# Second pass of a hybrid decoder step: the transposes of the normed rows inside v's projection instead of in front of it

## The reference: what is computed

```python
def trunk_layer(x, p, conv_buf, C0, n0, m0, lp):
    mix, new_state = parallel_mixer(rmsnorm(x, g_mix), ...)   # mLSTM heads and chunk MLP, then W_out
    h = x + mix
    h = h + hier_moe(rmsnorm(h, g_ffn), ...)                  # routed experts
    h = h + jax.nn.sigmoid(h @ w_pg) * rmsnorm(p @ w_ple_l, ple_g)
    return h, new_state

def chunk_mlp(u, v, w_s_l, b_s_l, vn_g):
    vn = rmsnorm(jax.nn.gelu(v).reshape(B, L, G_B, DG_B), vn_g.reshape(G_B, DG_B))
    z = jnp.einsum('gts,bnsgc->bntgc', w, vn.reshape(...)) + b_s_l[:, :Lc].T[:, :, None]
    out = jax.nn.gelu(u) * z.reshape(B, L, W_B)
    return out, vn.reshape(B, L, W_B)
```

## Time and profile before

| | |
|---|---|
| median of three runs | 2383.95 us |
| the profiled execution, its own time | 2384.98 us |
| its span in the trace | 2383.4 us |
| TensorE busy (matmuls) | 2200.5 us, 92% |
| VectorE busy | 1491.1 us, 63% |
| ScalarE busy | 973.5 us, 41% |
| GpSimd busy | 466.9 us, 20% |
| DMA, mean over the span | 171 GB/s |
| mean granted TensorE clock | 0.957 |

### The profile page before, as it was taken

The page is one execution under the profiler, slowest core; times in us unless marked ns, Lnnn a source line. Parts: engine busy times, 40 slices in busy tenths (PEclk is TensorE's granted clock), DMA queues, the critical chain, the costliest instruction groups (busy, mean ns, idle before and its releaser), DMA issues. The chain is left out here.

```text
span 2383.4 us, 34278 instructions
## 1 busy us (share of the span) xinstructions
PE 2200.5 (92%) x10675; PEld 1809.1 (76%) x10676; DVE 1491.1 (63%) x2827; ACT 973.5 (41%) x1567; POOL 466.9 (20%) x617
## 2 busy tenths in 40 slices
PE   7999988999699999998398999999999999969998
PEld 5888877788578788887277888878888888747775
DVE  5787787877635544554545467486664666835654
ACT  4334332343422222222344457376654665723332
POOL 1121443221112322322100000000000000023332
PEclk9999988999899999998699999999999999989999
DMA  6102112112523322321577577698775779844331
GB/s 219 62 32 82 62 40 97 40 62 98 177 74 100 115 102 98 115 100 45 213 295 278 221 266 291 244 347 295 294 296 219 272 286 349 300 168 143 134 142 59
DMA packets 159158, 407.04 MB, mean 171 GB/s; under 512 B 18700, under 2 KB 22212, under 8 KB 158847
## 3 DMA queue, kind: packets, MB, share of 16 engines
q1 hardware_dynamic: 137350, 337.15, 39.1%
q0 software_dynamic: 14560, 43.11, 5.4%
q10 hardware_dynamic: 7200, 26.22, 2.7%
HBM read 330.10 MB, written 84.82 MB: 174 GB/s over the span
## 5 line engine op out<-in xcount | busy, mean ns | idle before, releaser
L1961 DVE TENSOR_TENSOR w_lo<-raw,w_hi 128x2048 fp32r<-128x2048 f32 x196 | 434.9, 2286 | 49.0 <-ACT w_hi L1897 49.0
L1897 ACT ACTIVATE w_hi<-raw 128x2048 fp32r<-128x2048 f32 x196 | 358.4, 1930 | 25.4 <-DMA raw<-in_w 25.4
L212 PE MATMUL bank<-w_hi,mix_x 128*128 128x512 f32 x816 | 340.2, 417 | 16.9 <-DMA first_s<-in_b_s 7.2
L213 PE MATMUL bank<-w_lo,mix_x 128*128 128x512 f32 x816 | 331.1, 406 | 0.0
L214 PE MATMUL bank<-w_hi,mix_x 128*128 128x512 f32 x816 | 330.1, 405 | 0.0
L1862 PE MATMUL bank<-w_hi,x_hi 128*128 128x512 f32 x784 | 306.0, 390 | 2.1 <-DVE x_lo L1953 2.1
L1864 PE MATMUL bank<-w_hi,x_lo 128*128 128x512 f32 x784 | 306.0, 390 | 0.0
L1863 PE MATMUL bank<-w_lo,x_hi 128*128 128x512 f32 x784 | 305.7, 390 | 0.0
L212 PEld LDWEIGHTS bank<-w_hi,mix_x 128*128 128x128 f32 x816 | 161.2, 197 | 51.2 <-DMA first_s<-in_b_s 7.3
L214 PEld LDWEIGHTS bank<-w_hi,mix_x 128*128 128x128 f32 x816 | 161.2, 197 | 36.1
L213 PEld LDWEIGHTS bank<-w_lo,mix_x 128*128 128x128 f32 x816 | 161.8, 198 | 32.1
(11 more groups left out here) (286 smaller groups left out, 4035.2 us busy)
## 6 DMA issues: line engine op xcount, KB each, us to landing
raw<-in_w SPq DMA_DIRECT2D x192, 1024.0 KB, 8.0
y_dram<-y_sb ACTq DMA_DIRECT2D x50, 512.0 KB
xT_dram<-mix_x SPq DMA_DIRECT2D x34, 512.0 KB, 3.4
mix_x<-xT_dram SPq DMA_DIRECT2D x34, 512.0 KB, 4.3
raw_all<-in_w_in SPq DMA_DIRECT2D x24, 512.0 KB, 5.7
x_sb<-in_x_prompt SPq DMA_DIRECT2D x16, 512.0 KB
xr_sb<-in_x_prompt SPq DMA_DIRECT2D x16, 512.0 KB
h_dram<-h_sb SPq DMA_DIRECT2D x16, 512.0 KB
```

Source lines behind the costliest of these rows:

```text
L212: pe.matmul(bank[:, :], x_hi[:, k, :], wh[:, k, :], start=(k == 0), stop=False)
L213: pe.matmul(bank[:, :], x_hi[:, k, :], wl[:, k, :], start=False, stop=False)
L1897: return act.activation(out, in_, ACT.Copy)
L1961: dve.tensor_tensor(w_lo[slot(j, m)][:, cols], raw[m][:, cols], w_hi[slot(j, m)][:, cols].bitcast(F32), ALU.subtract).then_inc(lo_ready, 1)
```

## The change

`project` gets an argument `between`, a function that it calls ahead of its fourth k step (k = 3). `project_vb` hands it on. In a step that has both a next tile and a tile before, `hn_transposes(u - 1)` is this function: its two waits and eight transposes now stand behind nine of the 24 matmuls of v's projection for tile u + 1. In step 0 there are no transposes of `hn`, in step 16 there is no projection, and the transposes stand alone as before. No instruction is added or taken away, and no other engine's order changes.

```diff
-                def project(pe, bank, s, piece=None):
+                def project(pe, bank, s, piece=None, between=None):
 
 
                     wh, wl = (b[s][:, :].rearrange("p (k n) -> p k n", k=KD) for b in (w_hi, w_lo))
                     for k in range(KD):
+                        if between and k == 3:
+                            between()
                         if piece is not None and k % 2 == 0:
                             pe.wait_ge(p_lo, piece + k // 2 + 1)
...
-                            def project_vb(u):
+                            def project_vb(u, between=None):
                                 if past(u, 0):
                                     pe.wait_ge(vb_in, u)
-                                project(pe, B, 1).then_inc(vb_mm, 1)
+                                project(pe, B, 1, between=between).then_inc(vb_mm, 1)
...
                                 if r == P:
                                     chunk_mlp(u)
-                                if past(u, 0):
+                                if r_next:
+                                    project_vb(u + 1, past(u, 0) and (lambda: hn_transposes(u - 1, r_last)))
+                                elif past(u, 0):
                                     hn_transposes(u - 1, r_last)
-                                if r_next:
-                                    project_vb(u + 1)
                                 mix_transposes(u, r)
```

## The result

The changed kernel takes 2370.34 us (median of four runs, 2369.91 to 2370.65); four runs of the kernel before had a median of 2385.99 us (2383.44 to 2389.0). The ratio is 0.9931, with a 95% interval of 0.9919 to 0.9944: 0.7% faster, 13 to 19 us. Forecast were 16.4 us and 2367.5 us, within 2363 to 2374. The forecast time started from 2383.95 us, the median of three runs; from the median of four, 2385.99 us, the same 16.4 us lead to 2369.6 us.

What follows compares the result with a forecast made beforehand. TensorE's order of work, waiting each step for `hn` in a ring, was taken as the bound. Waits worth 18.2 us less 1.8 us for the break gave -16.4 us, 2383.95 to 2367.5 us, range 2363 to 2374.

Steps and rivals of the forecast that it cites:

- the ring: Second pass: logits through residual sum and norm to `hn` (19.0 us), then TensorE to logits (9.1 us), set the 28.16 us period.
- the two chains behind the stream: After the change, logits to `idx` (16.8 us) gives a period of about 26.95 us; the `hn` ring needs 26.1.
- (1): Nine projection matmuls bring TensorE to the transposes 3.05 us after the chunk MLP's start; `hn` allows 2.21, covering the wait.
- (2): Waits for `hn` removed: step 2 1.20 us, steps 3 to 14 1.33 us each, step 15 1.00 us; sum 18.2 us.
- (3): Breaking v's projection for the transposes costs 0.12 us a step, 1.8 us in all.
- (4): Chunk MLP's wait for `idx` binds next: 0.03 us remain, new period about 26.95 us.
- (5): Users of the later transposes stay in time; copies of `hnT` have 2.0 us to spare before `mix`'s transposes; costed at nothing.
- (6): After the pass, the experts' stage starts behind a barrier, so the gain of 16.4 us is passed on whole.
- in whole or half: Rivals: `hn` wait returns elsewhere, whole 2385.8 us (0.06, shared with no effect) or half 2376 us (0.05).
- fall at the break: Slower rival: clock drops for the 15 matmuls behind the transposes, +27 us, 2411 us; chance 0.03.
- The rule of the Trainium skill: Transposes within v's projection might pull the granted clock down, giving the slower rival's time, 2411 us.

Runs made afterwards that it cites:

- k = 1: Changed kernel with the `hn` transposes behind three matmuls of v's projection (one k step) instead of nine; steady period 27.48 us.
- swap_before: Kernel before, TensorE untouched, VectorE making the residual sum ahead of v's norm, ScalarE waiting for its gelu squares; 2364.38 us, period 26.73 us.
- less_after: Changed kernel without six of the output projection's 48 matmuls; period 26.92 us.
- less_swap_before: swap_before without six of the output projection's 48 matmuls; period 26.48 us.
- the split one: Changed kernel with the eight `hn` transposes in four pairs ahead of k steps 3 to 6; steady period 0.06 us longer.
- swap_after: Changed kernel with VectorE's residual sum moved ahead of v's norm and ScalarE waiting for its gelu squares; period 26.77 us.
- k = 6: Changed kernel with the `hn` transposes behind eighteen matmuls (six k steps) instead of nine; period 26.90 us.
- k = 7: Changed kernel with the `hn` transposes behind 21 matmuls (seven k steps) instead of nine; period 27.55 us.
- less_before: Kernel before without six of the output projection's 48 matmuls; one run 2394.48 us beside 2387.84 us for the kernel before.

## Why the prediction was right, point by point

**What bounds, and the ring: shown.** k = 1 ran at the ring's figure less three spacings, swap_before removed the wait without touching TensorE, and less_after and less_swap_before found the two chains behind the stream where they were placed.

**(1) The move covers the wait: shown.** Arrival 3.08 us behind the chunk MLP for 3.05; `hn` was finished 2.06 us behind it; the forecast counted 2.21 us, the start of the transposes that had waited for it.

**(2) The worth of the waits: right.** The intervals fell by 1.20 us (step 2), by 1.24 us in the steady steps and by 0.94 us (step 15), and the last interval by nothing. With the break of (3) taken off, the forecast had 1.08, 1.21 and 0.88 us. So the pass gained 16.95 us for 16.4. Of the 0.5 us between them, 0.10 and 0.12 come from steps 1 and 2, where the break is bare, 0.06 from step 15 and the rest from the steady ones, 0.03 at most each.

**(3) The break: mis-sized.** Forecast 0.12 us, measured 0.02 us where step 1 shows it bare (25.46 against 25.44), 0.03 us between the swap kernels and 0.03 to 0.04 us in the split one. The term that failed is the 0.92 us from the chunk MLP to the first wide matmul. It came from rows 5, where the chunk MLP itself had stood for `vn`. In an unbroken stream it is 0.81 us, in the timeline of swap_after:

```profile
853.34 1.05 PE L1346 MATMUL bank<-vn,wst 128*128 128x128 f32 x8
854.15 0.48 PE L214 MATMUL bank<-w_hi,mix_x 128*128 128x512 f32 x1
```

In a steady step of the changed kernel nine matmuls, transposes and fifteen matmuls take 861.24 - 853.85 = 7.39 us together (7.36 forecast), so there the error doesn't show. In swap_after they take 7.26 us. The difference belongs to (4).

**(4) What is late next: right place, undersized.** The chain through `idx` does bound the changed kernel, by the forecast's own sum: 880.79 - 863.98 = 16.81 us from the logits' end to the chunk MLP (16.8 forecast) and 863.98 - 853.85 = 10.13 us from there to the logits' end (10.14). The `idx` in question is that of two tiles back, not of the tile before, as the forecast says; it is made in the step before, so the sum is the same. But its price was put at 0.03 us, the delay of the chunk MLP's start. Here are the weight loads of the chunk MLP, in the changed kernel and in swap_after, where `idx` is early:

```profile
853.85 0.97 PEld L1346 LDWEIGHTS bank<-vn,wst 128*128 128x128 f32 x8 [0.31 <-DVE idx L1618]
```

```profile
853.12 1.08 PEld L1346 LDWEIGHTS bank<-vn,wst 128*128 128x128 f32 x8
```

In swap_after the first weight load starts 0.22 us ahead of the first matmul (853.34); behind the wait both start together. The chunk MLP then starts 0.28 us behind the last wide matmul instead of 0.23, and the next wide matmul comes 854.76 - 853.85 = 0.91 us behind it instead of 0.81. These 0.05 and 0.10 us are the whole difference of the periods, 26.92 - 26.77 = 0.15 us. The length of the wait hardly matters: behind stands of 1.25 us in less_after it is 0.91 to 0.92 us as well, and in k = 6, where the weight load waits for 0.2 us and the matmul isn't late at all, it is still 0.85 us.

So the two errors nearly cancel. The forecast's 26.95 us is step 1's 26.73, the 0.12 us of the break and 0.10 us by which a steady step exceeded 26.73 + 1.33, of which only 0.03 us were explained. Measured are 26.73, 0.03 for the break and 0.15 for the wait: 26.91 us, and the trace has 26.92. The late first wide matmul was in the forecast, but charged to the break instead of to the wait. That the errors cancel is luck; the mechanism is not.

**(5) The later transposes: shown.** The 2.0 us of room for the copies of `hnT` were right to a tenth; k = 6 came to the edge, and k = 7 used them up: its transposes of `mix` came 0.72 us late (0.7 expected) at the place named.

**(6) Behind the pass: as said.** From step 16's transposes of `hn` to the experts' first transposes it is 59.29 us before and 58.99 us after.

**The rivals.** The wait didn't come back, in whole or half. The clock didn't fall at the break: it is 1.00 from 672 to 1090 us. Of the two causes weighed for a fall, transposes in a projection and TensorE standing, less_before speaks for the second: the wait that the change removes, with one more like it and no break in the projection, went with a fall in half of the steady steps. The rule of the Trainium skill ("TensorE: Matmul & The Clock Gate", Part 4: PE-mode transpose) that transposes don't engage the full clock has no support here: with one set and even four pairs of them in a projection the clock stayed full, and the eight let the next wide matmul in after 0.79 us, as fast as in rows 4. No run here has a longer row of transposes alone, so what they do to the clock by themselves is not shown.

## What to carry to other kernels

When an engine waits in every step of a pipelined loop, find the ring that the wait closes: its length, less what is moved out of it, predicts the new period to a few hundredths, and the chain that is ready only just in time says how far it will help. The wait can be removed at either end, so look also at the engine that makes the late value: here VectorE stood for 3.4 us with the inputs of a later step ready, and the swap there gave a pass 4.8 us shorter than the move's. Take the price of an instruction's start from a place where the stream hasn't just stood, and look at the weight loads too: a wait can cost time there that the matmul rows don't name.

## What the runs showed of the hardware that was not expected

- Removing TensorE's work can cost time: with stands of 1.27 and 1.04 us on both sides of the chunk MLP the granted clock fell to its lower level in about every second step, 1.6 us each, and the pass grew from 446.97 to 455.18 us.
- Small matmuls (128 columns) in a stream of wide ones cost 0.02 to 0.04 us a break, though the follower of the first wide one starts 0.08 us late.
- A wait that delays TensorE's small matmuls by 0.05 us costs 0.15 us. It holds back their weight loads, which otherwise start 0.22 us ahead, and the first wide matmul behind them comes 0.91 us after them instead of 0.81.
